# Column sums of the trunk's norms: from sums in rows and a spread, to sums on all partitions

## The reference

```python
def rms_norm(x, g):
    xf = x.astype(F32)
    y = xf * lax.rsqrt(jnp.mean(xf * xf, axis=-1, keepdims=True) + EPS)
    return (y * g.astype(F32)).astype(x.dtype)
...
            h = rms_norm(x, norm_g[l, 0]) * (1 + sc1) + sh1
            ...                      # m = even_mixer(h, ...) or odd_mixer(h, ...)
            x = x + g1 * rms_norm(m, norm_g[l, 1])
            h = rms_norm(x, norm_g[l, 2]) * (1 + sc2) + sh2
            x = x + g2 * rms_norm(mlp(h, mlp_w1[l], mlp_w2[l]), norm_g[l, 3])
```

## Time and profile before

| What | Value |
|---|---|
| Median of three runs | 3595.27 us (3594.14 to 3598.88) |
| The profiled execution | 3591.43 us; its span, first to last instruction, 3589.8 us |
| TensorE busy, its weight loads | 3171.7 us (88%), 2783.1 us (78%) |
| VectorE, ScalarE, GpSimd busy | 1320.4 us (37%), 951.1 us (26%), 628.1 us (17%) |
| Mean granted clock of TensorE | 0.927 of full speed |
| Line 849, the sums, busy on TensorE | 21.4 + 9.7 us |
| Line 858, the spreads, busy on TensorE | 24.0 us |

### The profile page before, as it was taken

The page is one execution under the profiler, slowest core; times in us unless marked ns, Lnnn a source line. Parts: engine busy times, 40 slices in busy tenths (PEclk is TensorE's granted clock), DMA queues, the critical chain, the costliest instruction groups (busy, mean ns, idle before and its releaser), DMA issues. The chain is left out here.

```text
span 3589.8 us, 44989 instructions
## 1 busy us (share of the span) xinstructions
PE 3171.7 (88%) x17605; PEld 2783.1 (78%) x17605; DVE 1320.4 (37%) x2055; ACT 951.1 (26%) x1404; POOL 628.1 (17%) x368
## 2 busy tenths in 40 slices
PE   4898888889777688899999998879778899999998
PEld 2883333369656478899999998867568899999997
DVE  4126651111297417322222227119516422222225
ACT  3016663200231224212122223213324212222211
POOL 1211111121000021221112221117021112222210
PEclk7899999989889589999999999989779999999998
DMA  5110005421231232111111122130242111111112
GB/s 210 53 48 20 1 25 175 153 65 47 100 107 54 78 109 74 48 42 36 40 47 47 47 85 70 52 109 5 66 128 67 43 45 47 47 47 47 41 36 106
DMA packets 236954, 238.89 MB, mean 67 GB/s; under 512 B 8003, under 2 KB 194807, under 8 KB 236565
## 3 DMA queue, kind: packets, MB, share of 16 engines
q1 hardware_dynamic: 221701, 205.73, 18.2%
q0 software_dynamic: 5120, 16.78, 1.5%
q10 hardware_dynamic: 10016, 14.78, 1.2%
HBM read 207.74 MB, written 29.99 MB: 66 GB/s over the span
## 5 line engine op out<-in xcount | busy, mean ns | idle before, releaser
L614 PE MATMUL PS<-trunk_x_hi,trunk_w_hi 128*128 128x364 f32 x2208 | 739.1, 335 | 87.1 <-DVE trunk_x_lo L1242 31.9
L615 PE MATMUL PS<-trunk_x_lo,trunk_w_hi 128*128 128x364 f32 x2208 | 736.3, 333 | 0.0
L616 PE MATMUL PS<-trunk_x_hi,trunk_w_lo 128*128 128x364 f32 x2208 | 735.2, 333 | 0.0
L831 POOL TENSOR_TENSOR trunk_w_lo<-trunk_w_raw,trunk_w_hi 128x1024 fp32r<-128x1024 f32 x128 | 307.0, 2398 | 1318.4 <-ACT trunk_w_hi L1009 1228.1
L614 PE MATMUL PS<-hidden,trunk_w_hi 128*128 128x364 f32 x1536 | 508.0, 331 | 0.0
L615 PE MATMUL PS<-hidden,trunk_w_hi 128*128 128x364 f32 x1536 | 505.9, 329 | 0.0
L616 PE MATMUL PS<-hidden,trunk_w_lo 128*128 128x364 f32 x1536 | 505.5, 329 | 0.0
L614 PEld LDWEIGHTS PS<-trunk_x_hi,trunk_w_hi 128*128 128x128 f32 x2208 | 423.6, 192 | 89.2 <-DVE trunk_x_lo L1242 32.4
L615 PEld LDWEIGHTS PS<-trunk_x_lo,trunk_w_hi 128*128 128x128 f32 x2208 | 423.7, 192 | 0.0
L616 PEld LDWEIGHTS PS<-trunk_x_hi,trunk_w_lo 128*128 128x128 f32 x2208 | 422.8, 191 | 0.0
L1260 DVE TENSOR_TENSOR M<-M,PS 128x364 f32<-128x364 f32 x336 | 178.3, 532 | 440.9 <-PE PS L616 440.9
(11 more groups left out here) (369 smaller groups left out, 4266.3 us busy)
## 6 DMA issues: line engine op xcount, KB each, us to landing
trunk_w_raw<-mlp_w SPq DMA_DIRECT2D x128, 512.0 KB
M<-cache_sb_k SPq DMA_DIRECT2D x64, 256.0 KB, 3.0
big<-cache_sb_v POOLq DMA_DIRECT2D x64, 256.0 KB, 3.3
x_scratch<-x_new ACTq DMA_DIRECT2D x9, 1456.0 KB, 5.9
hgrn_pairs_ada_w<-ada_w SPq DMA_DIRECT2D x24, 512.0 KB
x_new<-x_scratch SPq DMA_DIRECT2D x6, 1456.0 KB, 11.8
trunk_x_old<-x_scratch SPq DMA_DIRECT2D x6, 1456.0 KB, 10.9
setup_ada_w<-ada_w SPq DMA_DIRECT2D x16, 512.0 KB, 7.2
```

The source lines that it names most:

```text
L614: pe.matmul(out, hi, xh, start=first, stop=False)
L615: pe.matmul(out, hi, xl, start=False, stop=False)
L616: return pe.matmul(out, lo, xh, start=False, stop=last)
L831: pool.tensor_tensor(wl[:, u % 4, :], raw[:, u % 2, :], wh[:, u % 4, :].bitcast(F32), ALU.subtract).then_inc(s_lo, 1)
```

## The change

In `trunk`, the sums are made with the operands exchanged. A column of ones, broadcast to 128 x 128, is the stationary operand, the squares are the moving one over 364 columns, and each column's sum appears on all 128 partitions, in the bank that the spread wrote before. The root is taken over 128 x 364 from PSUM into the new tile `rows` in SBUF, one half for n = 0 and one for n = 1, and the reciprocal in place there. `spread` and its semaphore go. `scaled` and `normed` read `rows` in SBUF where they read PSUM. In chunks 1 and 2 the wait for the earlier reader moves from TensorE's `sums` to ScalarE's `root`. In `norm_step`, some sums come one step sooner, where spreads stood: the sums of n = 0 for chunk 1 (second pair: before down tile 3 of chunk 2 instead of behind it, except in layer 1) and for chunk 2.

```diff
-        rt = sb("rt", [TB, 2, 2 * NBK])
-        rstd = sb("rstd", [TB, 2, 2 * NBK])
+        rows = sb("rstd", [P, 2, CW])
...
                 pe.wait_ge(s_tree[j][n], 2 * (c + 1))
                 if c:
                     pe.wait_ge(s_rt[j][n], c)
-                    if n == 0:
-                        pe.wait_ge(s_t[j], c)
-                    else:
-                        pe.wait_ge(s_y[j], 2 * c)
-                sq = squares_of(j, n, c)
                 for k in range(2):
-                    for b in range(4):
-                        q = pe.matmul(PS[0:TB, 6 + n, SUM_AT + 4 * c + b:SUM_AT + 4 * c + b + 1],
-                                      sq[:, k, b * TB:(b + 1) * TB], cols(core, "ones"), start=(k == 0 and b == 0), stop=True,
-                                      skip_group_check=True)
+                    q = pe.matmul(PS[:, 6 + n, 0:CW], cols(core, "ones").to_broadcast([P, P]), squares_of(j, n, c)[:, k, :],
+                                  start=(k == 0), stop=(k == 1))
                 q.then_inc(s_ss[j][n], 1)
 
-            def spread(j, n, c):
-                pe.wait_ge(s_rs[j][n], c + 1)
-                for b in range(4):
-                    at = NBK * n + 4 * c + b
-                    q = pe.matmul(PS[:, 6 + n, b * TB:(b + 1) * TB], rstd[:, j, at:at + 1].to_broadcast([TB, P]),
-                                  cols(core, "ident")[0:TB, 0:TB], start=True, stop=True)
-                q.then_inc(s_bc[j][n], 1)
-
             def norm_step(j, phase, s):
 
-                if phase == 1:
-                    if s == 2:
-                        sums(j, 0, 0)
-                    if s == 3:
-                        spread(j, 0, 0)
-                if phase == 2 and not (final and j):
-                    if s == 1:
+                if phase == 1 and s == 2:
+                    sums(j, 0, 0)
+                if phase == 2:
+                    if s == 1 and not (final and j):
                         sums(j, 1, 0)
                     if s == 2:
-                        spread(j, 1, 0)
-                    if s == 3:
                         sums(j, 0, 1)
...
                 if phase == 3:
                     if s == 4:
                         sums(j, 1, 1)
                     if s == 5:
-                        spread(j, 1, 1)
-                    if s == 6:
                         sums(j, 0, 2)
-                    if s == 7:
-                        spread(j, 0, 2)
-                if phase == 4:
-                    if s == 6:
-                        sums(j, 1, 2)
-                    if s == 7:
-                        spread(j, 1, 2)
+                if phase == 4 and s == 6:
+                    sums(j, 1, 2)
...
             if final:
                 sums(1, 0, 2)
-                spread(1, 0, 2)
...
             def root(j, n, c):
                 act.wait_ge(s_ss[j][n], c + 1)
-                act.activation(rt[:, j, NBK * n + 4 * c:NBK * n + 4 * c + 4], sums_at(n, c), ACT.Sqrt, scale=1.0 / D,
-                               bias=cols(core, "eps")[0:TB, :]).then_inc(s_rt[j][n], 1)
+                if c:
+                    act.wait_ge(s_y[j] if n else s_t[j], 2 * c if n else c)
+                act.activation(rows[:, n, :], PS[:, 6 + n, 0:CW], ACT.Sqrt, scale=1.0 / D,
+                               bias=cols(core, "eps")).then_inc(s_rt[j][n], 1)
...
             def recip(j, n, c):
                 dve.wait_ge(s_rt[j][n], c + 1)
-                at = slice(NBK * n + 4 * c, NBK * n + 4 * c + 4)
-                dve.reciprocal(rstd[:, j, at], rt[:, j, at]).then_inc(s_rs[j][n], 1)
+                dve.reciprocal(rows[:, n, :], rows[:, n, :]).then_inc(s_rs[j][n], 1)
 
             def scaled(j, c):
-                dve.wait_ge(s_bc[j][0], c + 1)
-                rows = PS[:, 6, 0:CW].unsqueeze(1).to_broadcast([P, KT, CW])
-                dve.tensor_tensor(col(M, c), col(M, c), rows, ALU.mult).then_inc(s_t[j], 1)
+                dve.wait_ge(s_rs[j][0], c + 1)
+                dve.tensor_tensor(col(M, c), col(M, c), rows[:, 0, :].unsqueeze(1).to_broadcast([P, KT, CW]),
+                                  ALU.mult).then_inc(s_t[j], 1)
...
             def normed(j, c):
-                dve.wait_ge(s_bc[j][1], c + 1)
+                dve.wait_ge(s_rs[j][1], c + 1)
                 dve.wait_ge(s_x2[j], 2 * (c + 1))
...
                     q = dve.scalar_tensor_tensor(out=M[:, k, lo:hi], in0=X[:, k, lo:hi], scalar=coef(scale[j])[:, k, 0:1],
-                                                 in1=PS[:, 7, 0:width(c)], op0=ALU.mult, op1=ALU.mult)
+                                                 in1=rows[:, 1, 0:width(c)], op0=ALU.mult, op1=ALU.mult)
```

More of the change, by code:

```diff
@@ L740, in trunk @@
             "m_normed", "x_new", "m_gated_samples", "y_out", "y_samples", "y_hi", "y_lo"))
-        s_q, s_tree, s_ss, s_rt, s_rs, s_bc = ([both(f"{n}{j}_") for j in range(2)] for n in (
-            "squares", "tree", "sumsq", "root", "rstd", "spread"))
+        s_q, s_tree, s_ss, s_rt, s_rs = ([both(f"{n}{j}_") for j in range(2)] for n in (
+            "squares", "tree", "sumsq", "root", "rstd"))
         PS = core.PS
@@ L841, in sums @@
                     pe.wait_ge(s_rt[j][n], c)
-                    if n == 0:
-                        pe.wait_ge(s_t[j], c)
-                    else:
-                        pe.wait_ge(s_y[j], 2 * c)
-                sq = squares_of(j, n, c)
                 for k in range(2):
-                    for b in range(4):
-                        q = pe.matmul(PS[0:TB, 6 + n, SUM_AT + 4 * c + b:SUM_AT + 4 * c + b + 1],
-                                      sq[:, k, b * TB:(b + 1) * TB], cols(core, "ones"), start=(k == 0 and b == 0), stop=True,
-                                      skip_group_check=True)
+                    q = pe.matmul(PS[:, 6 + n, 0:CW], cols(core, "ones").to_broadcast([P, P]), squares_of(j, n, c)[:, k, :],
+                                  start=(k == 0), stop=(k == 1))
                 q.then_inc(s_ss[j][n], 1)
-            def spread(j, n, c):
-                pe.wait_ge(s_rs[j][n], c + 1)
-                for b in range(4):
-                    at = NBK * n + 4 * c + b
-                    q = pe.matmul(PS[:, 6 + n, b * TB:(b + 1) * TB], rstd[:, j, at:at + 1].to_broadcast([TB, P]),
-                                  cols(core, "ident")[0:TB, 0:TB], start=True, stop=True)
-                q.then_inc(s_bc[j][n], 1)
-            def norm_step(j, phase, s):
-                if phase == 1:
-                    if s == 2:
-                        sums(j, 0, 0)
-                    if s == 3:
-                        spread(j, 0, 0)
-                if phase == 2 and not (final and j):
-                    if s == 1:
+            def norm_step(j, phase, s):
+                if phase == 1 and s == 2:
+                    sums(j, 0, 0)
+                if phase == 2:
+                    if s == 1 and not (final and j):
                         sums(j, 1, 0)
                     if s == 2:
-                        spread(j, 1, 0)
-                    if s == 3:
                         sums(j, 0, 1)
-                    if s == 4:
-                        spread(j, 0, 1)
-                if phase == 2 and final and j:
-                    if s == 2:
-                        sums(j, 0, 1)
-                    if s == 3:
-                        spread(j, 0, 1)
                 if phase == 3:
@@ L1220, in normed @@
                     sh = core.mod[:, shift[j][0], :].rearrange("p (f c) -> p f c", c=SEGP)[:, shift[j][1]:shift[j][1] + KT, 1:SEG]
-                    dve.tensor_tensor(w, X[:, :, SEQ:T], PS[:, 7, PW:PW + NS].unsqueeze(1).to_broadcast([P, KT, NS]),
+                    dve.tensor_tensor(w, X[:, :, SEQ:T], rows[:, 1, PW:PW + NS].unsqueeze(1).to_broadcast([P, KT, NS]),
                                       ALU.mult).then_inc(s_ys[j], 1)
```

2 lines of the change are left out of this document (removed).

## The result

The changed kernel takes 3615.94 us in the median of 11 runs, the kernel before 3595.27 in as many of the same rounds: 1.0046 times as long (95% interval 1.0031 to 1.0061), so some 16.5 us slower; the two medians stand 20.7 us apart (1.0057), which the interval takes in. The forecast was 3606 with a range to 3615; the median lies 0.9 us above it, 3595.27 x 1.0046 = 3611.8 within it. The profiled execution took 3616.41 us, its span 3614.8, at a mean granted clock of 0.921.

What follows compares the result with a forecast made beforehand. VectorE's queue was taken to set the pace in the norms, TensorE elsewhere. First pairs +8.0, second pair +3.3 and last norm -0.5 gave +10.8 us: 3602 for the profiled execution, 3606 for the median, range 3590 to 3615.

Steps and rivals of the forecast that it cites:

- The first rival: Norms: TensorE sets the pace, so spreads and idle time come back, 37 us at most, 3558 us; chance 0.09.
- that the stops fail to come: Rival, first and second pairs of norms: GpSimd finds VectorE at the reciprocal, one stop in each pair, 3596 us; chance 0.25.
- the third, with worse stops and a slower clock: Rival: each stop wakes another wait, TensorE falls to 1.2 GHz in each pause; over +18, 3617 us; chance 0.06.
- two or three stops ... between them: First pair, chunk 0: GpSimd stops VectorE for 4.3 or 6.45 us, taken as 5.35, together +4.85 us.
- 3.3 of 4.4: Second pair, layer 0: +4.4 us with all three GpSimd stops, 2.2 less for each that goes; +3.3 taken.
- only the last of eight instructions: First pair, chunk 0: the first GpSimd operation meets just the end of normed, so stops were taken as 5.35 us.
- forecast +4.85: First pair, chunk 0, up to chunk 1's sum: -0.5 us without stops plus 5.35 for two or three stops.
- where I took 1.9: First pair, chunk 1's sum to its low part: a gain of 2.6 or 1.2 us by clock, from VectorE's wait.
- The maximum near 2.7: Sign: the lines of normed and scaled show a longest instruction near 2.7 us, over GpSimd operations.
- The wait ahead of chunk 0: Sign, first pair: TensorE's wait for the low part, none before the change, should be 3 to 6 us.
- That at chunk 2: Sign, first pair: TensorE's wait for the low part, 10.6 us before, should stay near 11.
- That chunk 1 adds nothing: Second pair, layer 0: this chunk costs nothing, since its reciprocals lie under the next tile.

Runs made afterwards that it cites:

- e1: Changed kernel with the reciprocal on 4 of the 364 columns, output not the reference's; 0.9948 of the kernel before.
- e4: Changed kernel with four products that nobody reads on TensorE where each of 20 spreads stood; 1.0056 of the kernel before.
- e2: Changed kernel with the reciprocal's result written to the sum's PSUM bank and the multiplications reading it there; 1.0010 of the kernel before.
- e11: Changed kernel with root and reciprocal in one ScalarE activation, rows still in SBUF, no VectorE reciprocal; 0.9931 of the kernel before.
- e10: Kernel before the change, with products that nobody reads in TensorE's own waits for the low part; 0.9998 of the kernel before.
- e5: Changed kernel with root and reciprocal in one ScalarE activation, in place in PSUM, no VectorE reciprocal; 0.9915 of the kernel before.
- e8: Changed kernel with root and reciprocal in one activation in PSUM, plus products that nobody reads in TensorE's waits; 0.9895 of the kernel before.

## Why the prediction came out as it did

**Where it was right.** The mechanism: VectorE's queue sets the pace of the norms (e1, e4), the reciprocal is 2.42 us and three quarters of what it adds counts (35.9 of 21 x 2.25 = 47 us, e1), TensorE's saving is mostly waited away (e4), and the second SBUF operand lets GpSimd stop VectorE (e2, e11). The first rival, TensorE's pace, falls with e4; that the stops fail to come falls with the timeline; the third, with worse stops and a slower clock, had the right kind of thing in it (nine stops, 0.80 behind a pause) but +15.7 and not over +18.

**The term that was mis-sized: the number of stops.** For a first pair I took "two or three stops ... between them", and for the second pair 3.3 of 4.4 "with all three". All three came, in each of the three pairs and in both profiles. With three, the prediction's own sum is 2 x (4.0 + 1.1) + 4.4 - 0.5 = +14.1 (3.3 above its +10.8; its text says some 4). Measured from the pair's first sum to the first product of the third chunk: A 105.68 - 99.84 = +5.84, C 104.95 - 99.84 = +5.11, B 108.72 - 104.44 = +4.28, with D's -0.6 together +14.6. The hedge rested on the first operation meeting "only the last of eight instructions" of `normed`. It came in the sixth, 2.9 us into the group (2757.18 against 2754.29), and stopped the seventh, and a stop cost its 2.1 to 2.2 us whichever instruction it met; the two others met `low`, which had moved under them.

**Point by point in a first pair** (C, less before, cumulated): at the sum of chunk 1's second norm +7.0 (A +6.5), forecast +4.85, with the third stop +5.95; at the product of chunk 1 +4.1 (A +3.6); at that of chunk 2 +5.1 (A +5.8). The first is some 0.6 to 1.1 above what three stops explain: behind a pause of 7.6 us 60 products took 12.1 us, 0.202 each, in place of 0.167 (window clock 0.80), ScalarE's activation on that tile held up the squares of x behind it, and VectorE's tree stood 1.51 us at 2781.29. Chunk 1 gained 2.9 where I took 1.9, even more than the end of 2.6: the wait of 2.69 ahead of the hidden step is gone (2798.43 has none). Chunk 2 cost 1.0 in C, as forecast, and 2.3 in A, where the 84 products behind chunk 1's pause ran at 0.199 and not 0.184 us each, 1.3 us in all. So that a first pair ends close to its sum with three stops (+5.1 and +5.8 against +5.1) is in part luck: what the slower clock added, chunk 1 gave back.

**Wrong in what it would show.** The maximum near 2.7 came for `normed` and not for `scaled`, which no operation met in the changed kernel (3.18 to 3.19 us). The wait ahead of chunk 0 was to be 3 to 6 us and is 7.6, by the third stop. That at chunk 2 was to stay near 11 and is 15.2: I had left out that TensorE no longer stands for the spread ahead of it. The spread's wait went into the next one; the sum doesn't change.

**The second pair** went as its sum with three stops: one in `normed`, two in the first low half (timeline of VectorE, then GpSimd, answering to the earlier trace rows):

```profile
2196.20 6.29 DVE L1191 SCALAR_TENSOR_TENSOR M<-x_new,coef,trunk_rstd 128x364 f32<-128x364 f32 x8
...
2205.57 6.38 DVE L1201 SCALAR_TENSOR_TENSOR trunk_x_lo<-M,mod,trunk_x_hi 128x364 fp32r<-128x364 f32 x4
...
2212.32 2.11 DVE L1201 SCALAR_TENSOR_TENSOR trunk_x_lo<-M,mod,trunk_x_hi 128x364 fp32r<-128x364 f32 x4
```

```profile
2196.95 2.60 POOL L820 TENSOR_TENSOR trunk_w_lo<-trunk_w_raw,trunk_w_hi 128x1024 fp32r<-128x1024 f32 x1 [4.00 <-ACT trunk_w_hi L966]
2205.61 4.94 POOL L820 TENSOR_TENSOR trunk_w_lo<-trunk_w_raw,trunk_w_hi 128x1024 fp32r<-128x1024 f32 x2 [6.06 <-ACT trunk_w_hi L966]
```

That chunk 1 adds nothing came out (+0.3 us), but not by the reason given, that its reciprocals lie under the next tile: with short ones (e1) the way from the first product of chunk 0 to that of chunk 1 is 2.6 us shorter. They count, at least in part, and the wait for the spread that went makes up for them; that the term came right was luck. The stretch ends 1.3 us later still than its sum, behind a pause of 14.1 us; that slower products are the reason is not shown, since B gave no clean run on the clock (e10). **The last norm** was -0.6 against -0.5. The -0.5 takes some -1.2 for chunk 1, which the prediction doesn't write out. Its terms answer to the earlier trace rows: the wait of 3.38 for the tile is down to 0.57, the tail's 2.11 before `scaled` is now the reciprocal:

```profile
3574.93 0.53 DVE L1223 TENSOR_TENSOR M<-M,PS 128x364 f32<-128x364 f32 x1 [0.57 <-PE PS L616]
...
3592.77 2.43 DVE L1154 RECIPROCAL trunk_rstd<-trunk_rstd 128x364 f32<-128x364 f32 x1 [3.48 <-ACT trunk_rstd L992]
3595.24 3.19 DVE L1158 TENSOR_TENSOR M<-M,trunk_rstd 128x2912 f32<-128x2912 f32 x1
```

**What the change cost and what it gave.** The runs e1 to e5 and e11 split it: without the long reciprocal and the second SBUF operand, the exchanged sums without a spread give 26 us (e5). The reciprocal over 364 columns on every partition costs 26 us with the rows in PSUM (e2 less e5) and 35.5 with them in SBUF (changed less e11); the SBUF operand 6.5 to 15.8, part of which is who gets in first (e2).

## What to carry to other kernels

To make a small result appear on all partitions at once saves a step of waiting, but every later step then works on the full width: cost it on the engine whose queue sets the pace, and let another engine do it in one instruction if it can. Before an operand moves from PSUM to SBUF, look which GpSimd operations run beside its reader; count as a stop each one that hangs on the same events, not the share that the old timeline shows, but as an upper end: in e2 GpSimd stood instead. Cut the spans at marks to see a 15 us effect in profiles whose other stretches wander by 20.

## What the runs showed that I had not expected

Products that nobody reads, put into TensorE's waits, shortened the norms by the profiles: in e8 the products behind the two filled pauses in C ran at 0.167 and 0.168 us where e5 had 0.200 and 0.184, the three pairs are 12.8 us shorter, and the two kernels differ by nothing else. In the kernel before the same edit gave no time that the ratio shows (0.9998, 0.9989 to 1.0006); its stretches are 4.1 us shorter, with a low clock in a new place in B. And a reciprocal is not stopped by GpSimd: it takes 2415 to 2430 ns into SBUF and 2426 to 2436 into PSUM in all 21 places, also in the three (changed kernel) and five (e2) where a GpSimd operation ran beside it.
